# Softmax denominators of the attention heads: ScalarE's log and exp with one Newton step of VectorE in place of VectorE's reciprocal in pieces

## What is computed

```python
def attend(q, k, v):
    s = jnp.einsum('bqhd,bkhd->bhqk', q, k).astype(jnp.float32) * (MLA_QK ** -0.5)
    p = jax.nn.softmax(s, axis=-1).astype(v.dtype)
    return jnp.einsum('bhqk,bkhd->bqhd', p, v)
```

## Time and profile before

| | |
|---|---|
| median of three runs | 3463.0 us (3459.47 to 3467.32) |
| the profiled execution | 3462.45 us, span 3460.3 us |
| TensorE busy | 3309.1 us (96%) |
| VectorE busy | 1878.2 us (54%) |
| ScalarE busy | 878.2 us (25%) |
| GpSimd busy | 373.9 us (11%) |
| TensorE's granted clock, mean of the span | 0.965 |
| the heads of layer 0, first to last exponential | 444.8 to 791.1 us |
| the heads of layer 1, first to last exponential | 2144.2 to 2490.5 us |

### The profile page before, as it was taken

One profiled execution on the slowest core, in us unless ns is written; L12 is line 12 of the kernel. 1 busy time (PEld: TensorE's weight loads), 2 busy tenths in 40 slices (PEclk: granted clock), 3 DMA queues, 4 the chain that ended last, 5 costly groups with the idle time before them and its releaser, 6 DMA issues. The chain is left out here.

```text
span 3460.3 us, 45084 instructions
## 1 busy us (share of the span) xinstructions
PE 3309.1 (96%) x18370; PEld 2969.6 (86%) x18370; DVE 1878.2 (54%) x3173; ACT 878.2 (25%) x1364; POOL 373.9 (11%) x294
## 2 busy tenths in 40 slices
PE   5999899999899999999989998999998999999998
PEld 4998766658799999999979986666697999999998
DVE  5894745546865556555467765455316444434443
ACT  3222445442311111111132224544413111111110
POOL 0010322212100000000010104222211000000000
PEclk7997999999999999999999888999999999999999
DMA  6310000014332222222021000000211111111111
GB/s 259 95 36 1 14 3 4 3 67 153 108 96 73 85 67 67 91 79 73 25 92 47 24 3 11 4 5 1 79 37 61 37 37 48 46 39 40 45 36 55
DMA packets 45093, 185.57 MB, mean 54 GB/s; under 512 B 5473, under 2 KB 8993, under 8 KB 43425
## 3 DMA queue, kind: packets, MB, share of 16 engines
q1 hardware_dynamic: 38048, 158.58, 13.2%
q0 software_dynamic: 6912, 25.17, 2.5%
HBM read 169.14 MB, written 14.59 MB: 53 GB/s over the span
## 5 line engine op out<-in xcount | busy, mean ns | idle before, releaser
L1169 PE MATMUL ps<-a_hi,gu_hi 128*128 128x384 f32 x2112 | 709.4, 336 | 17.7 <-POOL a_lo L2296 6.4
L1169 PE MATMUL ps<-a_hi,gu_lo 128*128 128x384 f32 x2112 | 707.9, 335 | 0.0
L1169 PE MATMUL ps<-a_lo,gu_hi 128*128 128x384 f32 x2112 | 707.9, 335 | 0.0
L725 PE MATMUL ps<-a_hi,w_halves 128*128 128x384 f32 x1992 | 412.3, 338 | 12.2 <-POOL a_lo L2296 4.4
L1169 PEld LDWEIGHTS ps<-a_hi,gu_hi 128*128 128x128 f32 x2112 | 398.4, 189 | 23.0 <-issue 8.8
L1169 PEld LDWEIGHTS ps<-a_lo,gu_hi 128*128 128x128 f32 x2112 | 398.4, 189 | 0.0
L1169 PEld LDWEIGHTS ps<-a_hi,gu_lo 128*128 128x128 f32 x2112 | 398.2, 189 | 0.0
L725 PEld LDWEIGHTS ps<-a_hi,w_halves 128*128 128x128 f32 x1992 | 350.2, 189 | 22.3 <-issue 7.5
L2198 DVE TENSOR_TENSOR at<-ps,sg 128x384 f32<-128x384 f32 x132 | 73.4, 556 | 525.2 <-ACT sg L1612 525.0
L1198 PE MATMUL ps<-g_hi,d_hi 128*128 128x384 f32 x1056 | 352.9, 334 | 4.3 <-DVE g_lo L2200 4.3
L1198 PE MATMUL ps<-g_hi,d_lo 128*128 128x384 f32 x1056 | 352.7, 334 | 0.0
(11 more groups left out here) (281 smaller groups left out, 4700.2 us busy)
## 6 DMA issues: line engine op xcount, KB each, us to landing
f_raw<-wgu SPq DMA_DIRECT2D x88, 512.0 KB, 4.4
diag<-wada_c POOLq DMA_DIRECT2D x48, 512.0 KB, 3.9
f_raw<-wdn SPq DMA_DIRECT2D x44, 512.0 KB, 4.3
w_raw<-win SPq DMA_DIRECT2D x32, 512.0 KB, 3.7
wada_o<-wada_b SPq DMA_DIRECT2D x24, 512.0 KB, 3.6
spill<-z SPq DMA_DIRECT2D x2, 4608.0 KB
z<-spill SPq DMA_DIRECT2D x2, 4608.0 KB, 14.5
w_raw<-wout SPq DMA_DIRECT2D x16, 512.0 KB, 4.5
```

The lines of the kernel that those rows point to most:

```text
L725: mm = MM(ps[:, 3 * (n % 2) + b, 0:BLK], w, a[:, k, b * BLK:(b + 1) * BLK], start=(k == 0 and first), stop=(k == KC - 1 and last))
L1169: mm = MM(ps[:, unit_bank(v, g) + part, 0:BLK], w, a[:, k, b * BLK:(b + 1) * BLK], start=(k == 0 and j == 0), stop=(k == KC - 1 and j == 2))
```

## The change

The inversion of `dens` is split between two engines. ScalarE gets a new function, `inverted`: for a part it waits for the eviction, and, as there is one buffer `yinv` of 512 columns for all parts, for VectorE to be done with the part before (`at_rec`). It writes `yinv` = exp(-ln(dens)) with two activations, one linked behind the other. VectorE's `inverses` waits for that (`at_lnx`) and makes one Newton step, y(2 - d y), with two `scalar_tensor_tensor` (STT) instructions over the whole part, linked, each of which reads `dens` and `yinv`.

The places: ScalarE has part 0 at step 13 of the odd head, part 2 at step 4 and part 1 at step 5 of the even head; for the last pair parts 2 and 1 come after the evictions and ahead of the three `yhigh`. VectorE has part 0 at step 15 of the odd head, behind both units of that step, part 2 at step 4, part 1 at step 6 behind the units.

```diff
+        yinv = sb("yinv", [P, 512], F32, s5)
...
+        at_lnx = sig("at_lnx", 3 * H // 2)
...
+                def inverted(pair, o):
+
+                    q0, n = PARTS[o]
+                    k = 3 * pair + (1, 3, 2)[o]
+                    act.wait_ge(at_ev.sem, at_ev.at(l, 6 * pair + 4 + o))
+                    if k > 1:
+                        act.wait_ge(at_rec.sem, at_rec.at(l, k - 1))
+                    own.link(A(yinv[:, 0:n], dens[:, q0:q0 + n], ACT.Ln))
+                    A(yinv[:, 0:n], yinv[:, 0:n], ACT.Exp, scale=-1.0).then_inc(at_lnx.sem, 1)
...
+                    if h % 2 and st == 13:
+                        inverted(h // 2, 0)
+                    if h and h % 2 == 0 and st in (4, 5):
+                        inverted(h // 2 - 1, 6 - st if st == 4 else 1)
...
+                inverted(H // 2 - 1, 2)
+                inverted(H // 2 - 1, 1)
...
-                def inverses(pair, o, first=0, last=8):
+                def inverses(pair, o):
 
                     q0, n = PARTS[o]
-                    if first == 0:
-                        dve.wait_ge(at_ev.sem, at_ev.at(l, 6 * pair + 4 + o))
-                    part = dens[:, q0 + first * n // 8:q0 + last * n // 8]
-                    ins = V.reciprocal(part, part)
-                    if last == 8:
-                        ins.then_inc(at_rec.sem, 1)
+                    dve.wait_ge(at_lnx.sem, at_lnx.at(l, 3 * pair + (1, 3, 2)[o]))
+                    part, y_ = dens[:, q0:q0 + n], yinv[:, 0:n]
+                    link(STT(part, part, -1.0, y_, ALU.mult, ALU.mult))
+                    STT(part, part, 2.0, y_, ALU.add, ALU.mult).then_inc(at_rec.sem, 1)
...
-                        if h % 2 and st >= 15:
-                            inverses(h // 2, 0, 2 * (st - 15) + j, 2 * (st - 15) + j + 1)
+                        if h % 2 and st == 15 and j:
+                            inverses(h // 2, 0)
...
-                    if h and h % 2 == 0 and 5 <= st < 9:
-                        inverses(h // 2 - 1, 1, 2 * (st - 5), 2 * (st - 5) + 2)
+                    if h and h % 2 == 0 and st == 6:
+                        inverses(h // 2 - 1, 1)
```

## The result

| | before | after |
|---|---|---|
| median of four runs each, us | 3461.4 (3459.47 to 3467.32) | 3491.4 (3490.27 to 3493.35) |
| profiled execution: time, span, us | 3462.45, 3460.3 | 3491.71, 3489.6 |
| mean granted clock of TensorE | 0.965 | 0.961 |

The ratio is 1.0082, with a 95% interval of 1.007 to 1.0094. The change makes the kernel 0.8% slower, by 29.3 us between the two profiled executions. Forecast were 14.1 us and 3477 us, in a range up to 3485: the direction was right, the size was not, and the time lies outside the range.

A forecast was written before the change was run, and what follows sets the result against it. TensorE, busy 96% of the span, was taken as the bound, waiting in the heads on round trips with VectorE's reductions. Terms of +7.05 us a layer, +14.1 in two layers, gave 3477 us, slower by 0.41%, range 3467 to 3485.

The forecast's parts named there:

- The rule of the round trip: In the heads' matmul-reduction chain, 0.61 us of each 1.09 us turn is VectorE's to give; cost = hold - 0.61 - 0.06.
- The collision: Heads 1, 3 and 5: part 0's STT pair and GpSimd wait for each other; hold 2.98 us, cost 2.31 us each.
- Heads 2 and 4: Pairs of parts 1 and 2 hidden behind waits for TensorE; removed reciprocals give back 0.19 us in each head.
- Head 6: Part 1's pair costs 0.76 us, part 2's makes a reduction 0.50 late; four removed reciprocals give back 0.19 each.
- ScalarE's passes: Log and exp at steps 13, 4 and 5 take a copy's time, 0.622 us for 512 columns, and are hidden.
- The end of the heads: After the last head, GpSimd's last `low` stays hidden with 0.3 us left; otherwise up to 0.5 us a layer.
- The sum: Whole kernel: per layer 3 x 2.31 + 0.50 + 0.76 - 1.14 = +7.05 us, two layers +14.1.
- The rival that gave the right number: Heads 1, 3 and 5: GpSimd keeps the port over unbroken operations; cost 4.54 us each, +27.5, 3490; chance 0.11.

The follow-up runs named there:

- e8: Changed kernel with part 0's STT pair in heads 1, 3 and 5 replaced by one reciprocal over 312 of 512 columns; 3479.48 us, 1.0043.
- e7: Changed kernel with part 0 at step 17, part 2 at step 5, part 1 in 256-column halves at steps 7 and 8; 3465.18 us, 1.0003.
- e10: Changed kernel plus spare TensorE matmuls in heads 1, 3 and 5, nine ahead of unit 23 and two ahead of unit 24; 3478.53 us, 1.0033.
- e6: Changed kernel with GpSimd leaving out the rotary part of its run for heads 3, 5 and 7; 3472.41 us, 1.0022.
- e1: Changed kernel with only part 0 in the new manner, parts 1 and 2 by reciprocals in pieces as before; 3491.35 us, 1.0081.
- e3: Changed kernel with part 0's STT pair in heads 1, 3 and 5 replaced by one reciprocal over 224 of 512 columns; 3474.65 us, 1.0031.
- e4: Changed kernel with part 0's STT pair in heads 1, 3 and 5 replaced by one reciprocal over 472 of 512 columns; 3492.17 us, 1.0086.
- e2: Changed kernel with only parts 1 and 2 in the new manner, part 0 by reciprocals in pieces as before; 3464.92 us, 0.9999.
- e5: Changed kernel with VectorE's pair of part 0 at step 17 of the odd head instead of step 15; 3463.75 us, 1.0.
- e9: Changed kernel plus eight spare TensorE matmuls ahead of the second half of step 16 in heads 1, 3 and 5; 3484.07 us, 1.006.

## Why the prediction was wrong, step by step

- **The rule of the round trip** (0.61 us free, cost = hold - 0.67): right. e8 measured 1.30 to 1.33 for a hold that gives 1.34, e7 hid 0.41 us without a trace.
- **The collision**: right. 1.85 and 1.19 us against 1.84 and 1.19, the reduction 3.47 after the last against 3.46, an odd head at full clock 2.36 to 2.40 (e10) against 2.31. The rule on the shared ports, which the prediction took from the Trainium skill (page "SBUF — State Buffer", section "Who interferes with whom"), held here: a VectorE instruction with two SBUF inputs and a GpSimd one that reads SBUF wait for each other whole, and the times above were worked out so. e6, where they don't meet, is the counter-sample.
- **Heads 2 and 4**: right. The pairs are hidden, -0.19 each was forecast, -0.15 to -0.19 came in e10. After itself shows 0.53 to 1.00, for the stretches at the lower clock reach into these intervals (the first ends at 542.3, and head 2's interval begins at 540.05).
- **Head 6**: the mechanism right, the size a little off. Timeline of VectorE after, layer 0, steps 4 and 6 (it answers rows 9):

```profile
746.00 0.29 DVE L2116 SCALAR_TENSOR_TENSOR dens<-dens,yinv 128x128 f32<-128x128 f32 x1 [0.62 <-ACT yinv L1540]
...
746.54 0.28 DVE L2105 TENSOR_REDUCE pmx<-ps 128x1 f32<-128x128 f32 x1
...
750.02 0.68 DVE L2116 SCALAR_TENSOR_TENSOR dens<-dens,yinv 128x512 f32<-128x512 f32 x1
750.74 0.69 DVE L2117 SCALAR_TENSOR_TENSOR dens<-dens,yinv 128x512 f32<-128x512 f32 x1
751.35 0.55 DVE L2105 TENSOR_REDUCE pmx<-ps 128x1 f32<-128x384 f32 x1
```

  I had taken 0.741 and 0.346 us from instructions of other forms (one reads PSUM as well, the other writes fp32r); this pair's take 0.68 and 0.29. So head 6 cost 0.38 to 0.40 at full clock (e10) and not 0.50, which is nothing beside the rest.
- **ScalarE's passes**: right. Log and exp of 512 columns take 0.63 each, the 0.62 of the copy, and nobody waited.
- **The end of the heads**: right, narrowly. GpSimd's last `low` and the six weight loads after (they answer rows 11):

```profile
815.70 1.29 POOL L2379 TENSOR_TENSOR a_lo<-tsum,a_hi 128x512 fp32r<-128x512 f32 x1 [0.33 <-ACT a_hi L1546]
...
816.72 1.05 PEld L727 LDWEIGHTS ps<-a_hi,w_halves 128*128 128x128 f32 x6
```

  `low` ends at 816.99, and the fourth load, at 816.72 + 3 x 0.175 = 817.24, is the one that needs it: 0.25 us to spare, where 0.3 was forecast.
- **The sum: here is the failed step.** It adds up by how much each reduction is late and lets every matmul behind take what it took before. That holds only if TensorE's clock stays. I had the idle time in my own figures (a hold of 2.98 us in place of a free 0.61), and went on to what is late next on VectorE, GpSimd and ScalarE, but never asked what an idle TensorE does to its own clock. The term was priced at nothing, without a row and without a bound. It is worth 8.1 us in the heads, and in the medians the changed kernel stands 3491.4 - 3478.5 = 12.9 us above e10, the difference outside the heads included.
- **The rival that gave the right number** (GpSimd keeps the port, 3490) was wrong. By it the first STT would have started only after both GpSimd operations and the pair held for 5.21 us; the hold measured is 2.99, forecast 2.98, and the turns are those of the forecast. That the time came near 3490 is due to the clock.

Was there a row that could have warned me? Yes. The trace of before has idle times of TensorE of about 2 us outside the heads, and the clock stretches behind them differ. At the start of the feed-forward of layer 0, before:

```profile
918.67 0.45 PE L1169 MATMUL ps<-a_hi,gu_hi 128*128 128x384 f32 x1 [1.98 <-POOL a_lo L2296]
...
919.10:922.50 3.40, 3.40 (x13) 3.40 (x12) 3.36 (x5) 1.29 (x2) 0.05 (x1) 0.50 0.02 5
```

Behind 1.98 us of idle time the clock fell to 0.50 for 3.4 us, though TensorE was busy all that time; the same happened at 1772.20, behind 2.06 us. Further on in the same feed-forward it did not happen. TensorE's matmul and the stretch behind it, before:

```profile
1722.49 0.45 PE L1198 MATMUL ps<-g_hi,d_hi 128*128 128x384 f32 x1 [2.16 <-DVE g_lo L2200]
...
1723.40:1726.80 3.40, 3.40 (x22) 3.40 (x21) 1.98 (x4) 2.66 (x3) 0.00 (x0) 1.00 0.35 142
```

and after:

```profile
1736.02 0.45 PE L1200 MATMUL ps<-g_hi,d_hi 128*128 128x384 f32 x1 [2.16 <-DVE g_lo L2216]
...
1737.00:1740.40 3.40, 3.40 (x13) 3.40 (x12) 1.36 (x3) 2.62 (x3) 0.00 (x0) 0.50 0.35 139
```

The same 2.16 us of idle time; before, the clock stayed at 1.00, and after it fell to 0.50 and cost 1.5 us. So the trace of before alone gave both bounds: 2 us of idle time can be free or bring a lower clock behind it. Both should have stood in the prediction, and the range would then have reached further up than 3485.

**What stays open.** The feed-forward has this stretch in both layers after, in e1, e3, e4 and e7, in one layer in e2 and e8, and in neither before, in e5, e6, e9 and e10. e2 and e7 have it without any loss in the heads, and e9 and e10 lack it with one. So the change in the heads does not decide it; whether one idle time of 2.16 us brings the lower clock varies from one execution to the next. It makes some 3 of the 6.8 us outside the heads. Another 1.5 us come from a third place: at 1815.4 TensorE has waited 1.93 us, and after has a stretch at 0.50 from 1815.5, where before has the same wait and none. Of the rest, about 1.7 us arise ahead of the heads in code that is the same, and that start varies by -1.7 to +4.8 us between the kernels here. What makes the difference within a kernel (six odd heads in e3 are alike, and three are hit) wasn't settled either.

## What to carry to other kernels

When TensorE waits longer for another engine, price two things: the wait, and the clock behind it, which in this kernel cost 0.34 us for each microsecond at half speed in the heads, and came to more than half as much again as the waits alone (8.1 on 14.46). Look at the granted clock in stretches of a few microseconds, for the 40 slices of the page don't show it. And before giving an engine's work to cheaper instructions, look for the place: the same pair cost 28 us between two round trips and nothing two steps later, and 23 us less of VectorE's busy time bought nothing that the runs can tell, for most of it had lain where nobody waited for VectorE.

## What the runs showed of the hardware

- In the heads, a wait of TensorE of 0.49 (e6) or 0.57 us (e3) ahead of unit 23 went with a lower clock in three of six places each, 1.12 us in four of six (e8), 2.12 to 2.16 us in all six (e4, after). Each time a second wait of 0.65 us followed a matmul later; alone, that second wait stands in heads 0 to 6 of before, at full clock. With the first filled and the second cut to 0.18 us there was no stretch (e10); with the first cut to 0.31 and the second left, the fall came behind both, in four of six (e9).
- Outside the heads the outcome varied: behind waits of 1.98 and 2.06 us before had a stretch at 0.50, behind 2.16 us it had none, and after had one.
- A stretch at the lower clock lasted 3.4 or 6.8 us in the heads and cost 1.2 to 1.7 us for each 3.4. Chains of round trips slowed from 1.09 to 1.33 us a turn and not to double: the unit's matmul went from 0.45 to 0.69 us, and VectorE's part (0.56) stayed.
- Two two-input instructions of VectorE took turns with GpSimd's unbroken operations, one each, at 1.85 and 1.19 us instead of 0.68 and 0.69; a reciprocal, with one input, took the time of its length beside the same GpSimd work (1.54, 2.09 and 3.09 us for 224, 312 and 472 columns, 6.2 ns a column).
